# Two score banks in turn, and scores issued one step ahead, in the MLA stage of a two-layer kernel

## The chip, the cores and the metric

One core of a Trainium2 chip runs the whole program. The metric is the device time of one execution in microseconds (us); the median of 3 runs of the kernel before is 1999.83 us (1999.37 to 2000.95).

## The reference

Two transformer layers of different kinds over 512 tokens of width 1024. Only one part of the second layer is touched here: causal attention with latent projections (MLA), eight heads, computed in fp32 (`q`, `k` have 128 plain and 64 rotary features, `v` has 128):

```python
q = (rms(cq) @ w_uq).reshape(B, S, 8, 192)
kv = (rms(ckv) @ w_ukv).reshape(B, S, 8, 256); k_nope, v = kv[..., :128], kv[..., 128:]
k = concat([k_nope, broadcast(krope)]); q, k = rms(q), rms(k)      # then rotary on the last 64
s = einsum('bqhd,bkhd->bhqk', q_block, k) * 192 ** -0.5            # query blocks of 128, causal
mo = einsum('bhqk,bkhv->bqhv', softmax(s), v) @ w_bm
mixed = sigmoid(gr) * a_ret + sigmoid(gm) * mo                     # gr, gm = h @ parts of w_in
```

## The kernel before, in words

The program is written by hand for five in-order engines that meet only at semaphores. TensorE writes eight PSUM banks of 512 fp32 columns. Weights come from HBM in units into `raw`; ScalarE rounds a unit to `w_hi` (the high split), VectorE subtracts to make `w_lo` (the low split), and each product of weights is three matmuls (high x high, high x low, low x high).

The MLA stage (`mla`, one function of this name for each engine: L1299 on TensorE, L2123 on ScalarE, L3076 on VectorE) works on two heads at a time, in four rounds `i`. A round has eight steps `n`, one for each block of 128 queries and each of the two heads; `s = 8 * i + n`. The scores of step `n` have `(n // 2 + 1) * 128` columns, so steps 6 and 7 have 512. What a step does:

- TensorE (L1452 to L1475): `turn_p(s-1)` transposes the scaled probabilities of the step before; `scores(i, n)` writes bank 4; then transposes of new q or k tiles (`turn_q`, `turn_k`, bank 7); two pieces of weight work, `piece(i, 2n)` and `piece(i, 2n+1)`; and `weigh(s-1)`, probabilities times values.
- The pieces of rounds 0 to 2 prepare the next pair of heads: pieces 0 to 3 are quarters of gate `ga` (bank 2), 4 to 7 the four token tiles of the kv projection and 8 to 11 those of the q projection (banks 0 and 1 in turn), 12 to 15 quarters of gate `gb` (bank 3). A projection waits until the tile two before it has left its bank. In round 3 the 16 pieces are quarters of the four gates `gm`.
- VectorE (L3180 to L3223): `peak(s)` adds the causal mask in the bank and takes the row maximum; `scaled(s)` multiplies the exponentials with the inverse of their sum; `values` and `q_rope` take their parts of a projection out of its bank; `k_scaled`, `k_turned` scale and copy key tiles; `low` and `head_low` round outputs; `split` is the low split, in steps 0, 2, 4 and 7 (6 in round 3).
- ScalarE (L2210 to L2241): `high(s-2)` copies outputs, `projected` squares and copies a projection out of its bank, `fetch(s-1)` copies the transposed probabilities, `exp(s)` makes the exponentials out of bank 4 once `peak(s)` is done, then `q_turned`, `sigmoid` with table loads around it in step 1, and `split`.

In steps 3 and 4 VectorE's `values(i+1, 2n-5)` and in steps 5 and 6 its `q_rope(i+1, 2n-9)` stand ahead of `peak(s)`; on ScalarE the matching `projected` stands ahead of `fetch` and `exp(s)`. The next units after the stage (`merge2`) use banks 7, 4, 5, 6, 0, 1, 2 and 3.

## Time and profile before

| | us |
|---|---|
| median of 3 runs | 1999.83 |
| profiled execution, span | 1999.3 |
| TensorE busy | 1967.7 (98%) |
| VectorE busy | 1044.6 (52%) |
| ScalarE busy | 793.5 (40%) |
| MLA rounds (from the first scores to the last weighing) | 1309 to 1482 of the span |

Times in rows are counted from the span's start. A row of the timeline gives start, duration, engine, line, operation, tiles and shapes, and in brackets how long the engine had been idle before it and what ended that. A matmul's duration includes a tail that runs under the next ones; what it costs is the distance to the next start.

### The profile page before, as it was taken

The page shows a single profiled execution, that of the slowest core. Times are in us where ns is not written, and L with a number is a line of the kernel's source. Part 1 is how long each engine was busy: PE and PEld are TensorE (multiplying, and loading weights), DVE is VectorE, ACT ScalarE, POOL GpSimd, SP SyncE. Part 2 cuts the span into 40 slices and gives each one's busy share as a digit, 9 for nine tenths or more (in the row PEclk, how much of TensorE's full clock was granted, in tenths as well). Part 3 has the DMA queues.
Part 4 walks back from the last instruction along what each step waited for, and adds up shares of the span by engine and source line. Part 5 has one row for each costly group of instructions (what it writes and reads, how often), then busy time and mean ns, then how long its engine had stood idle before and what let it go on. Part 6 is the DMA issues. An engine that isn't in the chain of part 4 may idle for free.

```text
span 1999.3 us, 24017 instructions
## 1 busy us (share of the span) xinstructions
PE 1967.7 (98%) x9144; PEld 1594.7 (80%) x9144; DVE 1044.6 (52%) x1663; ACT 793.5 (40%) x1335; POOL 115.0 (6%) x138
## 2 busy tenths in 40 slices
PE   7999999999999999999999999999999999999998
PEld 6778777888888888877878787777778888888887
DVE  5687877455433544455353534466653553334354
ACT  5343556534222323333232323577752332322243
POOL 2140000002000000200000000000000200000011
PEclk9999999999999999999999999999999999999999
DMA  9842222123333332322223231211223332323321
GB/s 364 325 169 85 64 65 84 64 85 88 86 94 95 105 99 72 124 85 72 97 63 105 63 105 53 65 55 44 57 93 105 127 106 85 105 85 104 94 95 64
DMA packets 196578, 199.64 MB, mean 100 GB/s; under 512 B 7547, under 2 KB 170448, under 8 KB 194064
## 3 DMA queue, kind: packets, MB, share of 16 engines
q1 hardware_dynamic: 192416, 175.15, 28.2%
q0 software_dynamic: 4080, 23.40, 3.0%
q8 instruction: 51, 0.84, 0.2%
q14 instruction: 31, 0.25, 0.0%
HBM read 194.33 MB, written 4.19 MB: 99 GB/s over the span
## 4 chain that ended last, share of the span: by engine, by line
PE 90%; ACT 4%; DVE 3%; issue 1%; DMA 1%; SPq 0%; DVEq 0%; ACTq 0%
PE bank L761 47%; PE bank L1263 4%; PE bank L1014 4%; PE bank L851 4%; PE bank L837 3%; PE bank L1513 3%; PE bank L726 3%; PE bank L1333 2%; PE bank L1069 2%; PE bank L1241 2%; PE bank L881 1%; PE bank L998 1%; PE bank L964 1%; PE bank L1252 1%; PE bank L1283 1%
## 5 line engine op out<-in xcount | busy, mean ns | idle before, releaser
L1629 ACT ACTIVATE w_hi<-raw 128x2048 fp32r<-128x2048 f32 (+4 forms) x165 | 285.1, 1729 | 434.3 <-PE bank L761 306.6
L2372 DVE TENSOR_TENSOR w_lo<-raw,w_hi 128x2048 fp32r<-128x2048 f32 (+4 forms) x163 | 336.8, 2066 | 146.9 <-ACT w_hi L1629 145.0
L761 PE MATMUL bank<-h_hi,w_hi 128*128 128x512 f32 x864 | 337.7, 391 | 0.0
L761 PE MATMUL bank<-h_hi,w_lo 128*128 128x512 f32 x864 | 336.4, 389 | 0.0
L761 PE MATMUL bank<-h_lo,w_hi 128*128 128x512 f32 x864 | 336.1, 389 | 0.0
L761 PEld LDWEIGHTS bank<-h_lo,w_hi 128*128 128x128 f32 x864 | 162.2, 188 | 34.3 <-issue 0.5
L761 PEld LDWEIGHTS bank<-h_hi,w_lo 128*128 128x128 f32 x864 | 162.2, 188 | 34.0
L761 PEld LDWEIGHTS bank<-h_hi,w_hi 128*128 128x128 f32 x864 | 162.2, 188 | 34.0 <-issue 0.5
L761 PE MATMUL bank<-u_hi,w_hi 128*128 128x512 f32 x256 | 100.9, 394 | 0.0
L761 PE MATMUL bank<-u_hi,w_lo 128*128 128x512 f32 x256 | 100.4, 392 | 0.0
L761 PE MATMUL bank<-u_lo,w_hi 128*128 128x512 f32 x256 | 99.4, 388 | 0.0
L3311 DVE TENSOR_TENSOR xT<-bank,xT 128x512 f32<-128x512 f32 x32 | 22.1, 691 | 93.1 <-PE bank L761 92.5
L761 PE MATMUL bank<-g_hi,w_hi 128*128 128x512 f32 x176 | 69.4, 394 | 0.0
L761 PE MATMUL bank<-g_hi,w_lo 128*128 128x512 f32 x176 | 69.0, 392 | 0.0
L761 PE MATMUL bank<-g_lo,w_hi 128*128 128x512 f32 x176 | 68.3, 388 | 0.0
L1988 ACT ACTIVATE ft<-bank 128x512 f32<-128x512 f32 x22 | 13.2, 598 | 132.0 <-PE bank L761 125.7
L2856 DVE TENSOR_TENSOR ft<-bank,ft 128x512 f32<-128x512 f32 x22 | 15.2, 690 | 94.0 <-ACT ft L1988 94.0
L3299 DVE TENSOR_TENSOR nt<-nt 128x512 f32<-128x512 f32 x32 | 20.7, 688 | 77.3 <-ACT nt L2302 75.7
L2302 ACT ACTIVATE nt<-bank 128x512 f32<-128x512 f32 x32 | 17.4, 597 | 104.0 <-PE bank L761 104.0
L761 PEld LDWEIGHTS bank<-u_hi,w_lo 128*128 128x128 f32 x256 | 48.1, 188 | 11.3
L761 PEld LDWEIGHTS bank<-u_lo,w_hi 128*128 128x128 f32 x256 | 48.0, 188 | 10.8
L761 PEld LDWEIGHTS bank<-u_hi,w_hi 128*128 128x128 f32 x256 | 48.1, 188 | 9.6
(562 smaller groups left out, 4057.1 us busy)
## 6 DMA issues: line engine op xcount, KB each, us to landing
raw<-in_w_in SPq DMA_DIRECT2D x49, 1024.0 KB
raw<-in_w_ff SPq DMA_DIRECT2D x44, 512.0 KB
raw<-in_w_up SPq DMA_DIRECT2D x16, 1024.0 KB
raw<-in_w_down SPq DMA_DIRECT2D x16, 1024.0 KB
raw<-in_w_o SPq DMA_DIRECT2D x8, 1024.0 KB
raw<-in_w_br SPq DMA_DIRECT2D x8, 1024.0 KB
raw<-in_w_in SPq DMA_DIRECT2D x13, 512.0 KB
raw<-in_w_ff SPq DMA_DIRECT2D x8, 768.0 KB
```

The source lines that it names most:

```text
L726: last = nc.tensor.matmul(dst, a, b, start=n == 0, stop=n == len(terms) - 1)
L761: last = nc.tensor.matmul(dst, a, b, start=k == n == 0, stop=k == last_k and n == 2)
L837: last = nc.tensor.matmul(bank[t][:], a, b, start=half == k == n == 0, stop=half == 1 and k == 3 and n == 2)
L851: last = nc.tensor.matmul(bank[t][:], a, b, start=half == k == n == 0, stop=half == 1 and k == 3 and n == 2)
L1014: last = nc.tensor.matmul(bank[6 + n % 2][:], a, b, start=k == i == 0, stop=k == KD - 1 and i == 2)
L1069: last = nc.tensor.matmul(bank[2 * pair + m][:], a, b, start=k == i == 0, stop=k == 3 and i == 2)
L1241: last = nc.tensor.matmul(bank[4 + vt][:, j * P:S], rv[:, j, vt * P:vt * P + P], rs_t[:, j, 0:S - j * P], start=j == 0, stop=j == QT - 1)
L1263: last = nc.tensor.matmul(bank[OUT_BANK[half][n]][:], a, b, start=k == m == 0, stop=k == 3 and m == 2)
L1333: last = nc.tensor.matmul(bank[dst][:], a, b, start=k == n == 0, stop=k == KD - 1 and n == 2)
L1513: last = nc.tensor.matmul(bank[at][:], a, b, start=k == m == 0, stop=k == KD - 1 and m == 2)
L1629: nc.scalar.activation(w_hi[:, slot, 0:width], raw[:, slot, 0:width], ACT.Copy).then_inc(hi_done, 1)
L2372: v.tensor_tensor(w_lo[:, slot, 0:width], raw[:, slot, 0:width], w_hi[:, slot, 0:width].bitcast(F32), ALU.subtract).then_inc(lo_done, 1)
```

## The change

The scores alternate between banks 4 and 3. On TensorE, `scores(i, n+1)` is issued between the two pieces of step `n` (only the first scores of a round stay where they were) and waits for the exponential two steps before it instead of one. The transpose of the fourth key tile moves from ahead of the pieces of step 2 to behind them. Gate `gb` moves from bank 3 to bank 0, where it waits for the third q tile to have left, and the fourth `gm` gate from bank 3 to bank 7; the bank numbers of `merge2` follow. On ScalarE `exp(s)` is first in its step, then `high`, `fetch` and `projected`. On VectorE `peak(s)` is first in its step, ahead of `low`, `values` and `q_rope`, and each `k_turned(i, n)` stands in step `n` for 1 to 3. No instruction is added or taken away.

```diff
--- before.py
+++ after.py
@@ -358,7 +358,9 @@
         def x_copies(kind, j, t):
 
             return 2 + 20 * j + {"q": (3, 6, 9, 14), "k": (11, 16, 18, 20)}[kind][t]
-        GM_BANK = (2, 0, 1, 3)
+        GM_BANK = (2, 0, 1, 7)
+        GR_BANK = (2, 0)
+        S_BANK = (4, 3)
         SPLIT_STEPS = ((0, 2, 4, 7), (0, 2, 4, 7), (0, 2, 4, 7), (0, 2, 4, 6))
         kv_bank, q_bank = ((0, 1, 2, 3), (0, 1, 0, 1)), ((4, 5, 6, 0), (0, 1, 0, 1))
 
@@ -1313,6 +1315,8 @@
                         else:
                             pe.wait_ge(sem("kvq_act"), 3 * max(8 * j + t - 1, 8))
                             pe.wait_ge(sem("kvq_dve"), max(8 * j + t - 1, 8))
+                            if t == 0:
+                                pe.wait_ge(sem("gr_out"), 2 * j)
                         last = mm3(bank[kv_bank[j > 0][t]][:], tokens(lkv, t), [w_tile(u % 2, k, 512, 0, 512) for k in range(2)])
                     else:
                         if j:
@@ -1336,12 +1340,15 @@
 
                 def gr_piece(j, m, r):
                     if r == 0:
-                        if j:
-                            pe.wait_ge(sem("gr_out"), 2 * j - 1 + m)
+                        if m:
+                            pe.wait_ge(sem("kvq_act"), 3 * (8 * j + (7 if j else 8)))
+                            pe.wait_ge(sem("kvq_dve"), 8 * j + (7 if j else 8))
+                        elif j:
+                            pe.wait_ge(sem("gr_out"), 2 * j - 1)
                         else:
-                            pe.wait_ge(sem("kvq_act"), 3 * (3 + m))
-                            pe.wait_ge(sem("kvq_dve"), 3 + m)
-                    gate_quarter(u_mla(("ga", "gb")[m], j), 2 + m, r)
+                            pe.wait_ge(sem("kvq_act"), 3 * 3)
+                            pe.wait_ge(sem("kvq_dve"), 3)
+                    gate_quarter(u_mla(("ga", "gb")[m], j), GR_BANK[m], r)
 
                 def gm_piece(n, r):
                     if r == 0:
@@ -1350,8 +1357,9 @@
                         elif n == 1:
                             pe.wait_ge(sem("kvq_act"), 3 * 32)
                             pe.wait_ge(sem("kvq_dve"), 32)
+                            pe.wait_ge(sem("gr_out"), 8)
                         elif n == 3:
-                            pe.wait_ge(sem("gr_out"), 8)
+                            pe.wait_ge(sem("x_copied"), x_copies("k", 3, 3))
                     gate_quarter(U0["mla"] + 16 + n, GM_BANK[n], r)
 
                 def piece(i, n):
@@ -1396,10 +1404,11 @@
                 def scores(i, n):
                     t, hh = divmod(n, 2)
                     w = (t + 1) * P
-                    pe.wait_ge(sem("c_exp"), 8 * i + n)
+                    to = bank[S_BANK[n % 2]]
+                    pe.wait_ge(sem("c_exp"), max(8 * i + n - 1, 0))
                     pe.wait_ge(sem("x_copied"), max(x_copies("q", i, t), x_copies("k", i, t)))
-                    nc.tensor.matmul(bank[4][:, 0:w], qn[:, hh, t * P:t * P + P], kn[:, hh, 0:w], start=True, stop=False)
-                    nc.tensor.matmul(bank[4][:, 0:w], qr[:, hh, t * P:t * P + P], kr[:, 0:w], start=False, stop=True
+                    nc.tensor.matmul(to[:, 0:w], qn[:, hh, t * P:t * P + P], kn[:, hh, 0:w], start=True, stop=False)
+                    nc.tensor.matmul(to[:, 0:w], qr[:, hh, t * P:t * P + P], kr[:, 0:w], start=False, stop=True
                                      ).then_inc(sem("c_scores"), 1)
 
                 def turn_p(s):
@@ -1454,11 +1463,9 @@
                         s = 8 * i + n
                         if s:
                             turn_p(s - 1)
-                        scores(i, n)
                         if n == 0:
+                            scores(i, 0)
                             turn_q(i, 3)
-                        if n == 2:
-                            turn_k(i, 3)
                         if n == 5 and i < 3:
                             turn_q(i + 1, 0)
                         if n == 6 and i < 3:
@@ -1466,20 +1473,23 @@
                         if n == 7 and i < 3:
                             turn_q(i + 1, 2)
                         piece(i, 2 * n)
+                        if n < 7:
+                            scores(i, n + 1)
                         piece(i, 2 * n + 1)
                         if s:
                             weigh(s - 1)
-                        if n < 2:
+                        if n < 3:
                             turn_k(i, n + 1)
                         if n == 7 and i < 3:
                             turn_k(i + 1, 0)
 
                 def first_tile(k0, k1):
+                    pe.wait_ge(sem("c_exp"), 31)
                     for k in range(k0, k1):
                         pe.wait_ge(sem("heads_split"), k + 1)
                         a_hi, a_lo = w_tile(U0["merge2"] % 2, k, 256, 0)
                         for m, (a, b) in enumerate(((a_hi, mo_hi[:, k, :]), (a_hi, mo_lo[:, k, :]), (a_lo, mo_hi[:, k, :]))):
-                            nc.tensor.matmul(bank[7][:], a, b, start=k == m == 0, stop=False)
+                            nc.tensor.matmul(bank[4][:], a, b, start=k == m == 0, stop=False)
 
                 pe.wait_ge(lo_done, U0["merge2"] + 1)
                 first_tile(0, 3)
@@ -2158,7 +2168,7 @@
                 def sigmoid(j, m):
                     act.wait_ge(sem("gr_used"), max(2 * j + m - 1, 0))
                     act.wait_ge(mm_done, u_mla(("ga", "gb")[m], j) + 1)
-                    nc.scalar.activation(nt[:, 4 + m, :], bank[2 + m][:], ACT.Sigmoid).then_inc(sem("gr_out"), 1)
+                    nc.scalar.activation(nt[:, 4 + m, :], bank[GR_BANK[m]][:], ACT.Sigmoid).then_inc(sem("gr_out"), 1)
                 def exp_table(c):
                     nc.scalar.activation(warm[:, c:c + 1], eps[:], ACT.Exp)
 
@@ -2167,7 +2177,7 @@
                     act.wait_ge(sem("c_max"), s + 1)
                     act.wait_ge(sem("c_turned"), max(s - 1, 0))
                     w, n = (t + 1) * P, s % 8
-                    nc.scalar.activation(probs[:, s % 2, 0:w], bank[4][:, 0:w], ACT.Exp, bias=cst[:, 8 + n:9 + n],
+                    nc.scalar.activation(probs[:, s % 2, 0:w], bank[S_BANK[s % 2]][:, 0:w], ACT.Exp, bias=cst[:, 8 + n:9 + n],
                                          scale=inv[:, s // 8 % 2, 8 + 2 * t + hh:9 + 2 * t + hh], accum_out=cst[:, 16 + n:17 + n]
                                          ).then_inc(sem("c_exp"), 1)
 
@@ -2210,13 +2220,13 @@
                 for i in range(4):
                     for n in range(8):
                         s = 8 * i + n
+                        exp(s)
                         if s >= 2:
                             high(s - 2)
+                        if s:
+                            fetch(s - 1)
                         if i < 3 and 3 <= n <= 6:
                             projected(i + 1, "kv" if n < 5 else "q", (2 * n - 5) % 4)
-                        if s:
-                            fetch(s - 1)
-                        exp(s)
                         if n == 0:
                             q_turned(i, 3)
                         if 5 <= n <= 6 and i < 3:
@@ -3132,8 +3142,9 @@
                     t, hh = divmod(s % 8, 2)
                     w, n = (t + 1) * P, s % 8
                     dve.wait_ge(sem("c_scores"), s + 1)
-                    own.step(v.tensor_tensor(bank[4][:, t * P:w], bank[4][:, t * P:w], tri[:], ALU.add))
-                    own.step(v.tensor_reduce(cst[:, n:n + 1], bank[4][:, 0:w], axis=AX, op=ALU.max, negate=True))
+                    at = bank[S_BANK[s % 2]]
+                    own.step(v.tensor_tensor(at[:, t * P:w], at[:, t * P:w], tri[:], ALU.add))
+                    own.step(v.tensor_reduce(cst[:, n:n + 1], at[:, 0:w], axis=AX, op=ALU.max, negate=True))
                     v.tensor_tensor(cst[:, 8 + n:9 + n], cst[:, n:n + 1], inv[:, s // 8 % 2, 8 + 2 * t + hh:9 + 2 * t + hh],
                                     ALU.mult).then_inc(sem("c_max"), 1)
 
@@ -3180,7 +3191,8 @@
                 for i in range(4):
                     for n in range(8):
                         s = 8 * i + n
-                        if s >= 26 and n != 2:
+                        peak(s)
+                        if s >= 26:
                             low(s - 2)
                         if i < 3 and 3 <= n <= 4:
                             values(i + 1, 2 * n - 5)
@@ -3190,19 +3202,12 @@
                             sums(i + 1)
                         if n == 7 and i < 3:
                             inverse(i + 1)
-                        if n == 1:
-                            k_turned(i, 1)
-                        if n == 2:
-                            k_turned(i, 2)
-                            if i == 3:
-                                low(s - 2)
-                        peak(s)
+                        if 1 <= n <= 3:
+                            k_turned(i, n)
                         if n == 0:
                             k_scaled(i, 2)
                         if n == 1:
                             k_scaled(i, 3)
-                        if n == 2:
-                            k_turned(i, 3)
                         if n == 7 and i < 3:
                             k_scaled(i + 1, 0)
                         scaled(s)
...
```

## Rows read from the trace of the kernel before

**Rows 1.** Windows: length, busy PE, PEld, DVE, ACT, POOL, PE clock, DMA share, GB/s.
```profile
1356.00:1402.00 46.00, 43.91 (x234) 35.83 (x233) 29.02 (x99) 34.76 (x103) 0.00 (x0) 1.00 0.20 57
```

**Rows 2.** Waits of the stage: who, for whom, us in total, times, longest.
```profile
ACT nt L2170 <- DVE cst L3137: 42.1, 25, 3.0
...
PE bank L1409 <- DVE nt L3144: 3.5, 7, 0.8
```

**Rows 3.** Timeline of TensorE, rounds 0 and 1.
```profile
1310.33 0.50 PE L1333 MATMUL bank<-h_hi,w_hi 128*128 128x512 f32 x1
...
1355.14 0.47 PE L1333 MATMUL bank<-h_hi,w_hi 128*128 128x512 f32 x1 [0.84 <-DVE w_lo L2372]
...
1359.68 0.47 PE L1333 MATMUL bank<-h_hi,w_hi 128*128 128x512 f32 x1
...
1362.53 0.38 PE L1416 MATMUL bank<-nt,vv 128*128 128x128 f32 x2
...
1363.18 0.60 PE L1401 MATMUL bank<-kn,trigs 128*128 128x256 f32 x2
...
1364.05 0.51 PE L1394 MATMUL bank<-ident,kt 128*128 128x128 f32 x3
...
1369.67 0.39 PE L726 MATMUL bank<-w_hi,lat_lo 128*128 128x512 f32 x1
1370.15 0.47 PE L726 MATMUL bank<-w_hi,lat_hi 128*128 128x512 f32 x1
...
1373.47 0.64 PE L726 MATMUL bank<-w_hi,lat_hi 128*128 128x384 f32 x1
...
1380.86 0.34 PE L726 MATMUL bank<-w_hi,lat_hi 128*128 128x384 f32 x1
```

**Rows 4.** Timeline of ScalarE, the same rounds.
```profile
1311.77 0.46 ACT L2170 ACTIVATE nt<-bank,cst,inv 128x128 f32<-128x128 f32 x1
...
1362.68 1.08 ACT L2161 ACTIVATE nt<-bank 128x512 f32<-128x512 f32 x2
1363.78 1.28 ACT L2163 ACT_TABLE_LOAD   x1
...
1366.04 0.28 ACT L2138 ACTIVATE kt<-bank 128x128 f32<-128x128 f32 x1
...
1367.12 1.16 ACT L1629 ACTIVATE w_hi<-raw 128x1152 fp32r<-128x1152 f32 x1
...
1369.41 0.38 ACT L2178 ACTIVATE nt<-bank 128x256 f32<-128x256 f32 x1
...
1371.46 0.27 ACT L2138 ACTIVATE kt<-bank 128x128 f32<-128x128 f32 x1
...
1376.08 0.32 ACT L2138 ACTIVATE qt<-bank 128x192 f32<-128x192 f32 x1
...
1377.25 1.05 ACT L1629 ACTIVATE w_hi<-raw 128x1024 fp32r<-128x1024 f32 x1
```

**Rows 5.** Timeline of VectorE, round 1.
```profile
1359.41 0.42 DVE L3129 COPY kn<-bank 128x256 f32<-128x256 f32 x1
...
1359.96 0.30 DVE L3135 TENSOR_TENSOR bank<-bank,tri 128x128 f32<-128x128 f32 x1
...
1366.39 0.35 DVE L3144 TENSOR_SCALAR nt<-nt,cst 128x256 f32<-128x256 f32 x1
...
1368.31 1.36 DVE L2372 TENSOR_TENSOR w_lo<-raw,w_hi 128x1152 fp32r<-128x1152 f32 x1
1369.59 0.42 DVE L3083 COPY vv<-bank 128x256 f32<-128x256 f32 x1
1369.92 0.29 DVE L3135 TENSOR_TENSOR bank<-bank,tri 128x128 f32<-128x128 f32 x1
...
1374.30 0.29 DVE L3135 TENSOR_TENSOR bank<-bank,tri 128x128 f32<-128x128 f32 x1
...
1377.39 0.29 DVE L3092 TENSOR_TENSOR turned_q<-bank,q_tabs 128x128 f32<-128x128 f32 x1 [0.56 <-ACT qt L2143]
```

More of the change, by code:

```diff
@@ L1495, in first_unit @@
                 def first_unit():
-                    for n, dst in enumerate((7, 4)):
+                    for n, dst in enumerate((4, 3)):
                         for k in range(6 * (n == 0), KD):
@@ L1520, in merge2_mm @@
                 pe.wait_ge(sem("gm_out"), 4)
-                unit(u + 3, (2, 3), mo)
+                unit(u + 3, (2, 7), mo)
                 pe.wait_ge(sem("mixed"), KD + 2)
-                unit(u + 4, (7, 4), h)
+                unit(u + 4, (4, 3), h)
                 pe.wait_ge(sem("mixed"), KD + 4)
@@ L2272, in merge2_epi @@
                 for n in range(2):
-                    sigmoid(nt[:, n, :], (7, 4)[n], mm_done, u + 5)
+                    sigmoid(nt[:, n, :], (4, 3)[n], mm_done, u + 5)
                 split(u + 6)
@@ L3243, in merge2_epi @@
                 dve.wait_ge(sem("gr_used"), 8)
-                mixed(u, 0, 7, gm[:, 0, :])
-                mixed(u, 1, 4, gm[:, 1, :])
+                mixed(u, 0, 4, gm[:, 0, :])
+                mixed(u, 1, 3, gm[:, 1, :])
                 split(u + 2)
@@ L3255, in merge2_epi @@
                 mixed(u + 3, 4, 2, nt[:, 0, :])
-                mixed(u + 3, 5, 3, nt[:, 1, :])
+                mixed(u + 3, 5, 7, nt[:, 1, :])
                 v.memset(small[:, 22:23], 0.0).then_inc(banks_free, 25)
```

## Prediction

> **What bounds the kernel now.** I read the table of windows first. In the MLA stage TensorE is the bound: in one round of 46 us it is busy 43.91 us at granted clock 1.00, VectorE 29.02 and ScalarE 34.76 [rows 1]. The change can only win back the remainder, some 2 us a round. The waits name it: ScalarE's exponential waits 42.1 us for the row maximum, which costs nothing by itself, and TensorE's transpose of the probabilities (`turn_p`, L1409) waits 3.5 us in 7 places for the scaled probabilities [rows 2]. The real delay is longer than such a row says. A 512-wide matmul is shown as 0.39 us but the next one starts 0.23 us later, so about 0.17 us of each idle gap is hidden under the last matmul's tail [rows 3]. The seven waits are then 3.5 + 7 x 0.17 = 4.7 us: about 0.96 before step 7 of rounds 0 to 2, 0.9 in two places of round 0 and 0.9 in two places of round 3.
>
> Three other losses are in a round. Piece 7 (the fourth kv projection) starts at 1370.15, 0.48 after its predecessor instead of 0.23, so 0.25 late; the first q matmul (1373.47) shows 0.64 us where its neighbours have 0.34, so 0.30 late [rows 3]. The first gate piece of the next round waits 0.84 (really 1.1) for `w_lo` at 1355.14.
>
> I call that piece start T0 and give all times of rounds 1 and 2 from it; steps are counted 0 to 7, a step has pieces 2n and 2n+1, and p7 is piece 7. The same piece starts 44.07 us apart in rounds 1, 2 and 3; the first of the three is shown [rows 3].
>
> **What is removed.** With scores(n+1) issued between the pieces of step n, the maximum, exponential and scaling of head-step n have one and a half steps of TensorE work as cover, instead of one. All seven `turn_p` waits go: -4.7 us. The late p7 and p8 are replaced by what I find below, so I take their 0.55 a round off as well, in round 0 too, though it may have up to 0.5 more there. The wait for `w_lo` at T0 stays. It hangs on `turn_k` of the next round, which ends a round: `k_turned`, `k_scaled` and the low split follow it on VectorE in the same order as before.
>
> **What is added on TensorE.** No matmul is new. A scores block costs 0.87 us at 256 columns (1363.18 to 1364.05 [rows 3]), so 0.43 per 128 columns. A switch from a narrow fp32 matmul to a weight piece costs 0.09: twelve matmuls of 0.23 are 2.76, and the pair of pieces from 1359.68 to 1362.53 took 2.85. After scores in the middle there is one switch more where they are narrow (three in a round), and one where `turn_p` now stands directly before the piece (step 4, and steps 4 to 7 of round 3): 3 x 4 + 7 = 19 x 0.09 = 1.7 us. Its bounds are 0 and 28 x 0.09 = 2.5. The Trainium skill (TensorE: Matmul & The Clock Gate, Step-by-step) says that TensorE pulls weight loads ahead of running matmuls. Taken alone it would make the switches free and the sum 1.7 lower; the 0.09 measured at 1359.68 speaks against that for narrow matmuls.
>
> **What is moved on ScalarE and VectorE.** This is the costly part. `exp(s)` now stands first in ScalarE's step and `peak(s)` first in VectorE's. The evacuation that TensorE needs for bank 1, `projected(kv,1)` on ScalarE and `values(1)` on VectorE, stood ahead of them in step 3. Now it stands behind `exp(3)`, thus behind `peak(3)`, thus behind the low split that ends VectorE's step 2, thus behind the high split that ends ScalarE's step 2. p7 writes bank 1 and waits for it. I follow this chain from the end of p3, the last piece of gate a, which ScalarE's sigmoid waits for:
> - matmul tail 0.17, one sigmoid 0.54 (half of 1.08), exp table, mo copy, fetch and exp(2) together 2.26 (1363.78 to 1366.04), projected(kv,0) 1.08 (1366.04 to 1367.12), high split 1.16 [rows 4]: 5.21
> - low split and its hand-over 0.04 + 1.28 (1368.31 to 1369.59), peak(3) and exp(3) with their hand-over 1.54 (1369.92 to 1371.46) [rows 4, 5]: 2.86
> - mo copy 0.16, fetch(2) 0.28 (0.38 less the usual overlap of 0.1), projected(kv,1) 1.08 and 0.12 to VectorE, values 0.42 and 0.14 to TensorE (1369.59 to 1370.15) [rows 3 to 5]: 2.20
> Sum 10.3 us. TensorE took 1370.15 - 0.25 - 1362.53 = 7.37 from the end of p3 to p7; now scores(2) (0.87) lies before it, scores(4) (1.30) within it, and three switches more: 8.07. **p7 starts 2.2 us late**, in each of the rounds 0, 1 and 2.
>
> From there the two engines take turns. Counted from values(1), p7 starts at 0.56. VectorE: values(1) 0.34, the copies of the last key tile 0.55 (1359.41 to 1359.96), scaled(3) 0.47 (0.35 at 1366.39 and its short reciprocal), values(2) 0.34, then peak(4) and exp(4) 1.78 (1374.30 to 1376.08): 3.48. ScalarE: copies 0.16 + 0.28, projected(kv,3) 1.08, q0 1.17 (1376.08 to 1377.25), high split 1.05: 7.22. VectorE: low split 0.04 + 1.14 (1.28 less an eighth, as it is narrower), peak(5) and exp(5) 1.78: 10.2. ScalarE: copies 0.16 + 0.38, projected(q,1) until VectorE starts 1.31 (1376.08 to 1377.39), then q_rope 0.88 and 0.14 to TensorE: 13.0 [rows 4, 5]. p11, the fourth q piece, waits for exactly this. TensorE from p7 to p11 was 10.71 (1370.15 to 1380.86), less 0.30 of waiting, less scores(4) 1.30, plus scores(6) 1.73 and 0.18: 11.0, so it is ready at 11.6. **p11 starts 1.4 us late.** Behind it there is slack: gate b's bank 0 is free by its step, and turn_p(6) and the key transpose that end the round come 0.4 to 0.5 us later than what they wait for.
>
> A third, smaller one: scores(2) needs the second key tile half a step earlier. Its copy started at T0 + 4.27 (1359.41), right behind the low split of step 0 [rows 5]. Now two more ScalarE copies (0.64) stand before that split, and peak(1) (0.74, an estimate: 1.54 less the exponential of 0.56, the hand-over of 0.1 and the narrower reduction's 0.13) before the copy itself (0.62 to its end, and 0.14 to TensorE): 6.41. TensorE is there at 4.54 (1359.68) + 1.43 + 0.15 = 6.12: 0.3 late. In round 0 exp(0) starts 1.44 after T0 (1310.33 to 1311.77 [rows 3, 4]) instead of the 0.62 of the other rounds, two copies and one `weigh` of 0.88 on TensorE are missing: 0.3 + 0.82 - 0.64 + 0.88 = 1.35 late.
>
> The Trainium skill (same page, Architectural detail) states that ScalarE and VectorE are strict FIFO. By that rule nothing overtakes the waiting `peak` or `exp`, as in the chains; the trace agrees: ScalarE sits idle ahead of exponentials 42.1 us.
>
> **The other moves cost nothing.** Gate b in bank 0 waits for q2's evacuation, out by the above before p12; kv0 in bank 0 waits for the sigmoid of gate b, which runs in the idle time before gate a's. Moving the fourth key tile to step 3 leaves it two steps before scores(6). Weight loads from HBM start at the low splits, later by at most the stalls, and in this stage no high split waits for a transfer. The last units only change bank names.
>
> **The sum.** Rounds 1 and 2: -0.96 - 0.55 + 0.3 + 2.2 + 1.4 + 0.1 (p9, which is due just as bank 1 comes free) + 0.36 (4 switches) = +2.85 each. Round 0: -0.96 - 0.9 - 0.55 + 1.35 + 2.2 + 1.4 + 0.1 + 0.36 = +3.0. Round 3 has no projections, hence no p7 or p11 stall: -0.9 + 0.3 + 0.6 = 0. Together +8.7 us. The profiled span is 1999.33 and the median of the runs 1999.83, 0.5 apart, so 1999.8 + 8.7 = **2008.5**.
>
> **Rivals.**
> 1. The stalls of the score chain go and none comes: ScalarE and VectorE run far enough ahead that p7 and p11 aren't late. It decides on whether the chain after p3 is under 8.07 instead of 10.3, and the next under 11.0. For it: both engines are idle over a fifth of the round. Against: the chain begins with a sigmoid that can't start before p3 ends. Then -4.7 - 1.65 + 1.7 = -4.6, **1995.2**; with the late scores(2) (1.3 + 3 x 0.3 = 2.2) kept, 1997.4. The Trainium skill (Perfetto Trace Analysis, Matmuls) advises to rotate independent matmul groups through different PSUM banks so that evacuation overlaps the next group; by that rule this rival is what happens. The trace bears it out for the score bank and against it for bank 1, whose evacuation is queued later. Chance 0.15.
> 2. Only the first stall is real, and p11's is absorbed, for instance since projected(q,1) is early: 8.7 - 3 x 1.4 = +4.5, **2004.3**. Chance 0.15.
> 3. The lag isn't made good by the end of a round, and reaches the next round's low split and turn_p(6) (margin 0.5) again: 1 to 2 us more a round, **2013**. Chance 0.08.
> My forecast, the three late starts as priced, within 2005 to 2012: 0.62.
>
> Range 1997 to 2012: it takes in rival 2, the upper half of rival 1's spread (the late scores(2), all switches priced), the bounds of the switches, and an error of 1 us a round on the chains. A measurement of this kernel can tell 0.2%, 4.0 us, from no change. Faster than 1995.8 needs rival 1 nearly whole: 0.08. Between: the rest of it and half of rival 2, 0.19. Slower: 0.73.
>
> **What the profile after would show.** The `turn_p` waits gone; instead L726 waiting for VectorE's `vv` copy (L3083 before) some 2 us, three times, and for q_rope's output (L3098 before) some 1.3 us, three times; a scores wait on `kr` in step 1; rounds of about 46.9 us where they were 44.06, round 3 unchanged. ScalarE's wait for the maximum concentrated in steps 3, 4 and 5, behind the splits. The forecast is wrong if p7 starts without a wait, or if the round is under 45 us.

## The result, and the profile after

The changed kernel took **2009.39 us** (median of four runs, 2008.39 to 2009.99), the kernel before 2000.37 (four runs, 1999.37 to 2000.95). The ratio is **1.0046 [1.0031, 1.006]**: slower by 9.0 us. Single executions of one kernel lie in two groups some 1.5 us apart (1999.4 and 2000.9 for the kernel before) that differ ahead of this stage (round 0 begins at 1308.6 to 1308.9 us of the span in the profiles of the lower group, at 1310.1 to 1310.6 in the others), so a difference of medians is good to about 0.7 us, and the lengths of the rounds tell it more exactly. In the page's summary (busy time, share of the span, instructions) TensorE's busy time is what it was, 1968.3 against 1967.7 us; the span grew from 1999.3 to 2008.2.

```profile
span 2008.2 us, 24023 instructions
...
PE 1968.3 (98%) x9144; PEld 1595.1 (79%) x9144; DVE 1042.3 (52%) x1663; ACT 791.8 (39%) x1335; POOL 115.0 (6%) x138
```

The windows of the four rounds, from first gate piece to first gate piece and for round 3 to the first tile of the next stage (columns as in [rows 1]):

```profile
1310.14:1357.75 47.61, 41.51 (x216) 33.40 (x217) 28.48 (x96) 33.23 (x96) 0.00 (x0) 1.00 0.15 46
1357.75:1405.19 47.44, 42.37 (x225) 34.32 (x225) 27.67 (x95) 32.61 (x97) 0.00 (x0) 1.00 0.17 46
1405.19:1452.65 47.46, 42.38 (x224) 34.30 (x225) 27.67 (x95) 32.61 (x97) 0.00 (x0) 1.00 0.17 47
1452.65:1490.60 37.95, 37.76 (x190) 30.09 (x190) 25.48 (x71) 21.51 (x49) 0.00 (x0) 1.00 0.34 103
```

Cut in the same way, the rounds before were 44.81, 44.07, 44.07 and 38.49 us. The changes are +2.80, +3.37, +3.39 and -0.54: together +9.0, which is the whole result. The waits name the places. First TensorE's own (who, for whom, us in total, times, longest; they answer to [rows 2]):

```profile
PE bank L728 <- ACT kt L2148: 6.9, 3, 2.3
PE bank L728 <- DVE qt L3108: 4.1, 3, 1.4
...
PE bank L1337 <- DVE w_lo L2382: 2.5, 3, 0.8
...
PE bank L1410 <- ACT nt L2180: 1.8, 4, 1.2
```

and the largest of all engines within the stage, ScalarE's exponential waiting for the maximum, where it was 42.1:

```profile
ACT nt L2180 <- DVE cst L3148: 54.8, 24, 3.5
```

L728 is the projection (L726 before), L1337 a gate piece, L1410 the first scores matmul. `turn_p` (L1418 now) is in no row: its seven waits are gone. Two rows of the projection took their place, 6.9 us in three and 4.1 us in three. TensorE in round 1, whose T0 is now 1357.75 (these rows answer to [rows 3]):

```profile
1357.75 0.47 PE L1337 MATMUL bank<-h_hi,w_hi 128*128 128x512 f32 x1 [0.84 <-DVE w_lo L2382]
...
1364.12 0.67 PE L1410 MATMUL bank<-kn,trigs 128*128 128x256 f32 x2 [0.19 <-ACT nt L2180]
...
1366.44 0.38 PE L1425 MATMUL bank<-nt,vv 128*128 128x128 f32 x2
...
1373.75 0.81 PE L1411 MATMUL bank<-kr,trigs 128*128 128x384 f32 x2
...
1376.87 0.47 PE L728 MATMUL bank<-w_hi,lat_hi 128*128 128x512 f32 x1 [2.31 <-ACT kt L2148]
...
1387.14 1.02 PE L1411 MATMUL bank<-kr,trigs 128*128 128x512 f32 x2
1389.52 0.41 PE L728 MATMUL bank<-w_hi,lat_hi 128*128 128x384 f32 x1 [1.36 <-DVE qt L3108]
```

p7 starts at 1376.87, 19.12 after T0, and its gap of 2.31 us is longer in truth: the scores matmuls of 1373.75 (384 columns) would have let it start at 1374.40, had they cost the 0.65 that the same pair takes to the next start at 1380.57; that makes it **2.47 us** late (the piece behind the pair at 1381.22 comes 0.72 later, but that piece is late itself, as the part on the mis-sized terms shows). p11 starts at 1389.52, 31.77 after T0, **1.52 us** late, scores(2) at 1364.12 are 0.36 late. The name of a releaser needs care: the row of 1364.12 names an exponential, but the one that scores(2) wait for was long over; what had just ended was the copy of the key tile (VectorE, L3140, 1363.69 + 0.28 = 1363.97).

The chain to p7 on ScalarE (answering to [rows 4, 5]):

```profile
1366.70 0.60 ACT L2171 ACTIVATE nt<-bank 128x512 f32<-128x512 f32 x1 [0.43 <-PE bank L1337]
1367.31 1.28 ACT L2173 ACT_TABLE_LOAD   x1
...
1370.66 1.16 ACT L1639 ACTIVATE w_hi<-raw 128x1152 fp32r<-128x1152 f32 x1
1374.10 0.56 ACT L2180 ACTIVATE nt<-bank,cst,inv 128x256 f32<-128x256 f32 x1 [2.29 <-DVE cst L3148]
...
1375.88 0.38 ACT L2153 ACTIVATE kt<-bank 128x256 f32<-128x256 f32 x1
```

and VectorE's part of it:

```profile
1371.85 1.36 DVE L2382 TENSOR_TENSOR w_lo<-raw,w_hi 128x1152 fp32r<-128x1152 f32 x1 [0.37 <-ACT w_hi L1639]
1373.12 0.29 DVE L3146 TENSOR_TENSOR bank<-bank,tri 128x128 f32<-128x128 f32 x1
...
1376.30 0.42 DVE L3093 COPY vv<-bank 128x256 f32<-128x256 f32 x1 [2.23 <-ACT kt L2153]
```

Sigmoid, table, exp(2), high split (1370.66) on ScalarE; low split (1371.85) and peak(3) (1373.12) on VectorE; exp(3) (1374.10), the copy of the projection (1375.88) on ScalarE; values(1) (1376.30) on VectorE; p7. Each starts when the one before it has ended; between exp(3) and the copy of the projection stand only two short copies and the projection's own two squares (`projected` squares a tile twice, L2148, and then copies it, L2153).

### The profile page after: what moved, and what is told of

Same layout as the page of the kernel before. It is cut to its first block, busy times and chain, and to the rows that moved or that the text cites. A ratio compares the mean times of both kernels' runs of the same rounds, so it can differ in the third digit from the quotient of the medians.

```text
span 2008.2 us, 24023 instructions
## 1 busy us (share of the span) xinstructions
PE 1968.3 (98%) x9144; PEld 1595.1 (79%) x9144; DVE 1042.3 (52%) x1663; ACT 791.8 (39%) x1335; POOL 115.0 (6%) x138
## 4 chain that ended last, share of the span: by engine, by line
PE 90%; ACT 4%; DVE 4%; issue 1%; DMA 1%; SPq 0%; ACTq 0%; DVEq 0%
PE bank L763 47%; PE bank L1265 4%; PE bank L1016 4%; PE bank L853 4%; PE bank L839 3%; PE bank L728 3%; PE bank L1523 3%; PE bank L1337 2%; PE bank L1071 2%; PE bank L1243 2%; PE bank L883 1%; PE bank L1000 1%; ACT w_hi L1639 1%; PE bank L966 1%; PE bank L1254 1%
## 5 line engine op out<-in xcount | busy, mean ns | idle before, releaser
L763 PEld LDWEIGHTS bank<-u_lo,w_hi 128*128 128x128 f32 x256 | 48.1, 188 | 10.8
```

The costliest lines, as they stand in the source:

```text
L763: last = nc.tensor.matmul(dst, a, b, start=k == n == 0, stop=k == last_k and n == 2)
```

## Experiments

The question is what makes p7 and p11 late: the shared bank, the order on ScalarE, the order on VectorE, or the place of the scores.

### 1. The evacuation ahead of exp again, on both engines or on ScalarE alone

e1 moves `projected` ahead of `exp` and `values`/`q_rope` ahead of `peak` in steps 3 to 6; e2 makes only ScalarE's move:

```diff
                         s = 8 * i + n
+                        if i < 3 and 3 <= n <= 6:
+                            projected(i + 1, "kv" if n < 5 else "q", (2 * n - 5) % 4)
                         exp(s)
...
-                        if i < 3 and 3 <= n <= 6:
-                            projected(i + 1, "kv" if n < 5 else "q", (2 * n - 5) % 4)
```
e1 has this on VectorE besides:
```diff
-                        peak(s)
-                        if s >= 26:
-                            low(s - 2)
                         if i < 3 and 3 <= n <= 4:
...
                             q_rope(i + 1, 2 * n - 9)
+                        peak(s)
+                        if s >= 26:
+                            low(s - 2)
```

> The kernel after, with one edit on each of two engines: in steps 3 to 6 of rounds 0 to 2 the evacuations (projected on ScalarE, values and q_rope on VectorE) stand ahead of exp and peak again. Banks and TensorE's order stay. Theory A (queued-behind chain: p7 and p11 wait because the evacuation stands behind exp and peak): the three waits of 2.3 us before p7 and the three of 1.4 us before p11 go; about 0.4 us comes back before p8, since kv2 is then due just after it. A round falls from 47.44 us to about 43.8, the kernel to 1998 to 1999.5. Theory B (the scores between the pieces cost the time by themselves, through switches of TensorE or the earlier need of the second key tile): 2007 to 2009, as the kernel after.

> The kernel after with ScalarE's edit of the run before alone; VectorE's values and q_rope stay behind peak. Theory A1 (ScalarE's queue is the link that matters: the projection's evacuation waits behind exp, exp waits for peak, peak for the low split): projected(kv,1) runs straight after the high split of step 2, values(1) is at T0 + 16.1 to 16.5 and p7 is ready at 16.8, so again 1998 to 1999.5. Theory A2 (VectorE's order is the link): values(1) behind peak(3) still holds p7, a wait of 1 us or more before p7 and p11 stays, 2003 or more.

Measured: **e2 1998.63 us, 0.9988 [0.9979, 0.9998]**; e1 2006.37, 1.0024 [1.0013, 1.0034]. The one move on ScalarE is worth 2009.39 - 1998.63 = 10.8 us (11.4 by the rounds, which are 43.82, 43.65, 43.66 and 37.96 in e2). In e2 the row for p7 and the row for p11 are gone and no row of waits came in their place; what is left there are starts that are 0.18 to 0.27 us late under the tail of the matmul ahead (p6, p7 and p8 of round 1). ScalarE of e2 shows why: the projection is taken straight behind the high split (its first square starts at 1366.72), and exp(3) still waits 1.22 us for its maximum after that, so the move cost the exponential nothing.

```profile
1365.66 1.16 ACT L1639 ACTIVATE w_hi<-raw 128x1152 fp32r<-128x1152 f32 x1
1366.72 0.27 ACT L2148 ACTIVATE kt<-bank 128x128 f32<-128x128 f32 x1
...
1369.12 0.56 ACT L2180 ACTIVATE nt<-bank,cst,inv 128x256 f32<-128x256 f32 x1 [1.22 <-DVE cst L3148]
```

e1 fell outside both expectations. p7 and p11 are on time there, but three others are late. TensorE's waits of e1:

```profile
PE bank L1337 <- ACT qt L2148: 2.3, 3, 0.8
...
PE bank L728 <- ACT kt L2148: 1.8, 3, 0.6
```

and VectorE's timeline of e1 in step 3 of round 1:

```profile
1372.26 0.42 DVE L3093 COPY vv<-bank 128x256 f32<-128x256 f32 x1
1372.59 0.29 DVE L3146 TENSOR_TENSOR bank<-bank,tri 128x128 f32<-128x128 f32 x1
```

The rows are gate b's first piece (0.77 late in round 1), and p8 (0.60); a weighing in step 7 waits 0.52 besides. With `values(1)` (1372.26) ahead of it, peak(3) begins at 1372.59, behind a copy. In steps 5 and 6 it is worse: `q_rope` waits for ScalarE's copy, and peak, which could have run meanwhile, waits with it; then exp waits for peak, and the copies behind exp wait for exp. The two engines run one after the other instead of side by side. So in the changed kernel the two moves have opposite signs: taking back exp's move on ScalarE gains 10.8 us, taking back peak's as well loses most of them again: 7.7 by the medians (2006.37 - 1998.63), 7.3 by the rounds (46.26, 46.07, 46.07 and 37.96 in e1).

### 2. A third bank instead

The tiles of the projections go through banks 0, 1 and 2 instead of 0 and 1 (bank 2 is free between the gates), everything else as in the changed kernel, apart from the waits that go with it:

```diff
-        kv_bank, q_bank = ((0, 1, 2, 3), (0, 1, 0, 1)), ((4, 5, 6, 0), (0, 1, 0, 1))
+        kv_bank, q_bank = ((0, 1, 2, 3), (0, 1, 2, 0)), ((4, 5, 6, 0), (1, 2, 0, 1))
...
-                            pe.wait_ge(sem("kvq_act"), 3 * max(8 * j + t - 1, 8))
+                            pe.wait_ge(sem("kvq_act"), 3 * max(8 * j + t - 2, 8 * j))
```

> The kernel after with three banks in turn (0, 1, 2) for the eight projection tiles of a pair instead of two, so that each piece waits for the tile three before it; all orders stay. Theory A (the chain through both engines is the bound, and the bank only the place where TensorE meets it): the waits before p7 and p11 go, but turn_p(4), turn_q(0) and p12, which need the same chain, take about 0.7, 0.8 and 1.3 us of waiting instead; 2006.5 to 2009, a gain of 0 to 3 us. Theory C (two banks are too few): all of 12 us comes back, 1997.5.

Measured: 2008.40 us, 1.0040 [1.0026, 1.0054], as theory A said. The waits of p7 and p11 are gone, and the time is all but the same, since others wait instead (waits, then one row of TensorE's timeline):

```profile
PE bank L1424 <- DVE nt L3161: 5.0, 5, 1.6
PE bank L1339 <- issue: 3.1, 4, 0.8
```

```profile
1377.99 0.44 PE L1424 MATMUL bank<-ident,nt 128*128 128x128 f32 x2 [1.55 <-DVE nt L3161]
```

L1424 is `turn_p`, L1339 a gate piece; the wait of 1.55 us at 1377.99 is for the scaled probabilities that ScalarE and VectorE had not yet reached. One more bank only lets TensorE run up to the next thing that the same late chain delivers. (The expectation put the wait one `turn_p` later than it stands.)

### 3. One step at a time

e7 puts `projected` ahead of `exp` in step 3 alone; e6 leaves the order and moves the split of the q weights, which stands in the chain to p7, from step 2 to step 3:

```diff
+                        if i < 3 and n == 3:
+                            projected(i + 1, "kv", 1)
                         exp(s)
...
-                        if i < 3 and 3 <= n <= 6:
+                        if i < 3 and 4 <= n <= 6:
```
```diff
-        SPLIT_STEPS = ((0, 2, 4, 7), (0, 2, 4, 7), (0, 2, 4, 7), (0, 2, 4, 6))
+        SPLIT_STEPS = ((0, 3, 4, 7), (0, 3, 4, 7), (0, 3, 4, 7), (0, 2, 4, 6))
```

> The kernel after with ScalarE's evacuation ahead of exp in step 3 alone (projected(kv,1)); steps 4 to 6 keep exp first. Theory A: p7's three waits of 2.3 us go, p11's stay at 1.1 to 1.5, the kernel is at 2001 to 2003. If p7's lateness covers another one (TensorE would only wait later), p11's wait grows by what p7's shrinks and the time stays at 2007 to 2009.

> The kernel after with the split of the q weights moved from the end of step 2 to the end of step 3 in rounds 0 to 2, on both engines. It takes 1.16 and 1.28 us out of the chain from the end of p3 to p7 and puts them into the chain from there to p11. If the chain is as written, the 2.3 us wait before p7 shrinks to under 0.3, p8 waits about 0.8 for the low split, and p11's wait grows from 1.4 to 2.3 or more; the time stays within 1.5 us of the kernel after. If the wait before p7 has another cause than the splits ahead of peak(3), it stays at 2.3.

Measured: e7 2006.41, 1.0028 [1.0016, 1.0040]; e6 2010.25, 1.0051 [1.0035, 1.0067]. TensorE of e7 in round 1:

```profile
1377.95 0.42 PE L728 MATMUL bank<-w_hi,lat_hi 128*128 128x384 f32 x1 [0.66 <-ACT qt L2148]
...
1385.54 0.41 PE L728 MATMUL bank<-w_hi,lat_hi 128*128 128x384 f32 x1 [1.37 <-DVE qt L3110]
```

and of e6:

```profile
1373.84 0.47 PE L728 MATMUL bank<-w_hi,lat_hi 128*128 128x512 f32 x1 [0.60 <-ACT kt L2148]
...
1377.03 0.44 PE L728 MATMUL bank<-w_hi,lat_hi 128*128 128x384 f32 x1 [0.89 <-DVE w_lo L2382]
...
1380.89 0.41 PE L728 MATMUL bank<-w_hi,lat_hi 128*128 128x384 f32 x1 [0.74 <-ACT qt L2148]
...
1388.48 0.41 PE L728 MATMUL bank<-w_hi,lat_hi 128*128 128x384 f32 x1 [1.40 <-DVE qt L3108]
```

In e7 p7 shows no wait, but p9 (1377.95) now waits 0.66 us and p11 (1385.54) still 1.37: of the 7.4 us that three late starts at p7 cost, 3.0 came back by the medians and 3.8 by the rounds (46.37, 46.16, 46.15), between the two figures that were expected. p11's lateness is its own, not p7's handed on. In e6 the wait of 2.31 at p7 became 0.60, 0.89 and 0.74 at p7, p8 and p9, and p11 comes 32.05 us after T0 (1356.43) instead of 31.77. So the wait at p7 shrank, as the chain demands, but not to the 0.3 that was expected, and p11's wait did not grow to 2.3: p8 and p9 took it up. Taking the split out of the one chain put it into the next: a round is as long as the work that ScalarE and VectorE do in turn, not as the one wait that shows.

### 4. The place of the scores and the second bank

e11 is the changed kernel with `scores(i, n)` back at the start of its own step (two banks, new orders). e4 is the kernel before with the new orders (one bank, `exp` first, `peak` first). e8 is the kernel before with `peak` first on VectorE alone.

```diff
+                        scores(i, n)
                         if n == 0:
-                            scores(i, 0)
...
                         piece(i, 2 * n)
-                        if n < 7:
-                            scores(i, n + 1)
```
e4, on ScalarE, against the kernel before:
```diff
+                        exp(s)
                         if s >= 2:
                             high(s - 2)
-                        if i < 3 and 3 <= n <= 6:
-                            projected(i + 1, "kv" if n < 5 else "q", (2 * n - 5) % 4)
                         if s:
                             fetch(s - 1)
-                        exp(s)
+                        if i < 3 and 3 <= n <= 6:
+                            projected(i + 1, "kv" if n < 5 else "q", (2 * n - 5) % 4)
```
e4 and e8, on VectorE:
```diff
+                        if n == 1:
+                            k_turned(i, 1)
+                        if n == 2:
+                            k_turned(i, 2)
+                        peak(s)
+                        if s >= 26:
                             low(s - 2)
...
-                        peak(s)
```

> The kernel after with both score banks and both orders kept, but scores(i, n) at the start of step n as before. With e4_order_alone (2045.7) it tells which part of TensorE's change keeps the new order from costing 45 us. Theory P (the place: issued a step ahead, the scores are finished before the evacuation that they queue ahead of is wanted): 2040 to 2047, as e4. Theory Q (the second bank, which lets the scores be written before the exponential of the step before is read): near the kernel after, 2009 to 2015.

> The kernel before with the new order alone: exp first in ScalarE's step, and peak ahead of low, values and q_rope in VectorE's; one score bank, scores at the start of their step. Theory A: p7 is 2.9 us late and p11 2.0 us late in three rounds, less the 0.55 of waits that they replace, and turn_p still waits: 1999.8 + 3 x 4.35 = 2013, between 2010 and 2015. Theory B (the scores' new place costs the time): 1999 to 2001.

> The kernel before with VectorE's order alone changed: peak(s) ahead of low, values and q_rope; one score bank, scores in their old place, ScalarE as before. It asks whether e2_act_only's gain over the kernel before is the two banks' or only VectorE's order. Theory A (the gain is the early scores'): turn_p(6)'s 0.96 goes three times, since peak(6) no longer stands behind q_rope, but p7 and p11 become some 0.9 and 0.3 us later three times: 1999 to 2002. Theory D (VectorE's order is the gain): 1997 to 1998.6.

| scores | ScalarE: projection behind exp | ScalarE: projection ahead of exp |
|---|---|---|
| a step ahead, two banks | 2009.39 (after) | 1998.63 (e2) |
| at the start of their step | 2045.64 (e11, two banks), 2045.68 (e4, one bank) | 2001.00 (e8, one bank; ratio 1.0001 [0.9991, 1.0010]) |

`peak` stands ahead of the evacuations on VectorE in all of them; in e8 `high` and `fetch` stand ahead of exp as well. e8 by itself changes nothing: the `turn_p` waits fall from 3.5 us in 7 places to 0.5 in 2, and p7 waits up to 1.0 us for `values`, which now stands behind `peak`. The ratio of e11 is 1.0224 [1.0208, 1.0239], that of e4 1.0225 [1.0208, 1.0242]. e4 missed its expectation by over 30 us: I had priced the lateness of p7 and p11 only. With the scores at the start of the step the ring closes: the copy out of the bank waits for exp, exp for peak, peak for the scores, and these for the late piece ahead of them on TensorE. The waits of e4's stage:

```profile
DVE bank L3135 <- PE bank L1402: 39.2, 18, 4.2
...
PE bank L726 <- ACT kt L2138: 10.9, 3, 3.6
PE bank L726 <- DVE qt L3098: 8.4, 3, 2.8
```

and a window of e11 that covers its round 1, and behind it the row of p7 in that round, of TensorE's timeline:

```profile
1369.00:1428.00 59.00, 46.56 (x224) 37.67 (x224) 28.30 (x95) 32.50 (x97) 0.00 (x0) 0.91 0.14 37
```

```profile
1388.25 0.76 PE L728 MATMUL bank<-w_hi,lat_hi 128*128 128x512 f32 x1 [3.61 <-ACT kt L2146]
```

VectorE waits 39.2 us in 18 places for scores. e11 and e4 agree to 0.04 us: **in the change's order the second bank by itself is worth nothing, and the place that it allows is worth 36 us**. Part of the 36 is a lower clock: over the four rounds TensorE is busy 178.07 us in e11 and 164.01 in the changed kernel, with the same matmuls (see the last part). With the projection ahead of exp, place and bank together (and with them the banks of the gates and the order of `high` and `fetch`, which differ between e8 and e2 too) are worth 2.4 (2001.00 against 1998.63); no run takes these apart.

### 5. What is left of e2's waits: the key copies

e2's remaining waits are `w_lo` at T0 (2.5 us, 3 times) and scores(2) (1.8, 4 times). e5 moves `k_turned(i, 1)` ahead of the low split of step 0, and `k_scaled(i+1, 1)` behind the low split of step 7. e9 leaves the splits first, puts `k_turned(i, 1)` ahead of peak(1), and moves `k_scaled(i, 1)` behind peak(0) of the next round; e10 makes that last move alone, in the kernel before.

```diff
                         s = 8 * i + n
+                        if n == 1:
+                            k_turned(i, 1)
                         peak(s)
...
                         if n == 0:
+                            if i:
+                                k_scaled(i, 1)
                             k_scaled(i, 2)
...
                             k_turned(i + 1, 0)
-                            k_scaled(i + 1, 1)
```

> The version of e2_act_only (ScalarE's evacuations ahead of exp, all else as after) with two more moves on VectorE: the copy of the second key tile goes from step 1 to the end of step 0, ahead of the low split, and the scaling of the next pair's second key tile goes behind the low split of step 7. What e2_act_only still waits for is scores(2) on the key copy (1.39 in round 0, 0.36 in rounds 1 to 3) and the first gate piece of a round on the low split (1.08 three times). Theory A (each of these is what ends its wait): 2.5 and 3 x 0.72 = 2.2 us go, 1998.6 becomes 1993 to 1995. Rival (the next thing on VectorE or ScalarE is late just behind them): 1997 or more.

> The version of e2_act_only with two moves on VectorE, placed where VectorE has nothing to wait for: the copy of the second key tile stands ahead of peak(1), still behind the low split of step 0, and the scaling of the next pair's second key tile moves from step 7 to step 0 of the round that needs it, behind peak(0), where VectorE was idle 2.0 us. Theory: e5_two_copies lost because its copy stood ahead of the low split and waited for TensorE's transpose, which held up peak(1), exp(1) and gate b's sigmoid; here 3 x 0.72 of the low-split wait at T0 and 3 x 0.36 + 0.7 of the scores(2) wait go, 3.9 us: 1994 to 1996 beside 1998.6. If exp(1), now 0.55 later, holds the sigmoid past piece 4: 1996 to 1998.

> The kernel before with one of these moves alone: the scaling of the next pair's second key tile behind peak(0). The low split at T0 comes 0.72 earlier in three rounds: 2000.9 - 2.2 = 1998.7, if nothing else ends the wait of 1.1 at T0; exp(0) is not delayed. So 1998 to 1999.5.

Measured: e5 1999.84, 0.9995 [0.9986, 1.0004]; **e9 1996.55, 0.9979 [0.9970, 0.9988]**; e10 1998.77, 0.9990 [0.9981, 0.9999]. VectorE of e5:

```profile
1358.15 0.42 DVE L3139 COPY kn<-bank 128x256 f32<-128x256 f32 x1 [2.30 <-PE bank L1402]
...
1358.69 1.22 DVE L2382 TENSOR_TENSOR w_lo<-raw,w_hi 128x1024 fp32r<-128x1024 f32 x1
1359.82 0.29 DVE L3146 TENSOR_TENSOR bank<-bank,tri 128x128 f32<-128x128 f32 x1
```

TensorE of e5, at p4:

```profile
1363.61 0.47 PE L728 MATMUL bank<-w_hi,lat_hi 128*128 128x512 f32 x1 [1.08 <-ACT nt L2171]
```

TensorE's waits of e9:

```profile
PE bank L1410 <- DVE kr L3140: 1.6, 4, 0.5
...
PE bank L1337 <- ACT nt L2171: 0.8, 1, 0.8
```

In e5 the copy stood first, waited 2.30 us for its transpose, and held up the low split and peak(1) behind it, thus exp(1) and the sigmoids; p4, which needs gate b's bank, waited 1.08 us, a gate piece of round 3 waited 1.7 for gate b's sigmoid, and the gain was gone, as the rival said. In e9 the same copy stands behind the split, where its transpose is ready. The row for `w_lo` at T0 is no longer in e9's list nor in e10's, and e10's round is 43.36 (T0 at 1352.93 and 1396.29) instead of 44.07: 3 x 0.71 = 2.1 us, beside 2.04 between the medians (2000.81 and 1998.77). e9 beats the kernel before by 4.3 us and the changed one by 12.8. What it has left is 0.8 us at a gate piece of round 3, which waits for gate b's sigmoid, and the key copies' 1.6. Against e2 it gained 2.1 us where up to 3.9 was expected: the first three rounds fell to 42.94, 42.90 and 42.93, but round 3 grew from 37.96 to 38.51.

## Why the prediction held, point by point

The mechanism is the one that was forecast, and the runs show it: late evacuations at p7 and p11. That the total came within 0.3 us (+9.0 against +8.7) is partly luck: the sum took away 1.0 us too little, added 2.9 too little for late starts and 1.7 for switches that cost nothing, and these cancel. This is the ledger of the four rounds, summed from the distances between starts in both traces. A start counts as late by what it exceeds the usual distance (0.23 us behind a 512-column piece matmul, 0.17 behind a 384-column one, 0.11 for each 128 columns of every other record; a row with x2 holds two records), and the first matmul behind a wait takes 0.07 to 0.08 more than its like, which belongs to the price.

| us, all rounds | forecast | in the traces |
|---|---|---|
| late starts taken away | -6.3 | -7.3 |
| late starts added | +13.4 | +16.2 |
| switches | +1.7 | 0 |
| sum | +8.7 | +8.9 |

- **What is removed.** All seven `turn_p` waits went, and so did the late start at p7; `w_lo` at T0 stayed at 0.84 (2.5 in three), as said. The second "late" piece, p8, was misread: in the kernel before, the scores matmul of 384 columns starts at 1373.12 and the second matmul of p8 at 1373.94, and 0.82 is just 0.65 + 0.17. The first matmul of p8 was not late; its record only begins early. What was late there was `turn_p(3)`, by 0.18. Round 0 had 0.8 more to lose than the sum took (the prediction said up to 0.5).
- **p7, forecast 2.2, measured 2.47.** The three parts of the chain were forecast at 5.21, 2.86 and 2.20. Measured they are 5.38 (p3's end at 1366.44 to the high split's end, 1370.66 + 1.16), 2.83 (to 1374.65, where exp(3) is done) and 2.22 (to 1376.87): 10.43. TensorE reached the place 7.96 after p3's end, not 8.07 (the three switches in that sum cost nothing, and a late start of p6, 0.18, is in the 7.96). Both misses point the same way. The first part's miss is the second sigmoid: from p3's end to the table load at 1367.31 are 0.87 where 0.17 + 0.54 = 0.71 was taken from half of a back-to-back pair.
- **p11, forecast 1.4, measured 1.52.** From values(1) 13.22 instead of 13.0, TensorE 11.70 instead of 11.6.
- **scores(2), forecast 0.3 and 1.35 in round 0, measured 0.36 and 1.39.**
- **Mis-sized terms.** Rounds 1 and 2 came 0.5 longer than the +2.85 of the sum. With the 0.07 or 0.08 behind each wait, p7 costs 0.34 more than its term, p11 0.20 and scores(2) 0.13. p9, priced at 0.1, shows no wait but is 0.15 late: its bank comes free when values(3) ends at 1381.79, and it starts at 1381.94. p6 is late in the same hidden way, by 0.18 (it starts at 1371.62, values(0) ends at 1371.48), and is not in the sum at all. That is 0.9 more, less 0.36 for switches that cost nothing. Round 0 came at +2.80 against +3.0, round 3 at -0.54 against 0.
- **The switches.** This term was mis-sized: 1.7 forecast, nothing measured. The 0.09 came from the first matmul of a piece, which takes 0.31 to the next start instead of 0.23. But it starts only 0.03 behind the start of the last narrow matmul, which alone costs 0.11. Over both, nothing is lost (round 0 of the changed kernel):

```profile
1311.64 0.38 PE L1410 MATMUL bank<-kn,trigs 128*128 128x128 f32 x2
1311.86 0.39 PE L1411 MATMUL bank<-kr,trigs 128*128 128x128 f32 x2
1312.00 0.48 PE L1337 MATMUL bank<-h_hi,w_hi 128*128 128x512 f32 x1
1312.31 0.39 PE L1337 MATMUL bank<-h_lo,w_hi 128*128 128x512 f32 x1
```

  A pair of narrow matmuls takes 0.22 (1311.64 to 1311.86), and pair and first piece matmul together take 0.45 (1311.86 to 1312.31) = 0.22 + 0.23. The kernel before has the same at the place that the prediction read: 0.45 from 1359.54 to 1359.99. It holds for wide scores too: step 5 of round 3 takes 4.83 in the kernel before (1465.10 to 1469.93) and 5.25 in the changed one (1475.20 to 1480.45), which has one switch more and 0.43 more of scores. So the prediction's 0.09 against free switches does not stand, and round 3 comes out to within 0.1: 1.06 us of `turn_p` waits went, 0.43 at scores(2) came, and the 0.6 of switches never did.
- **The rivals.** The first (no late start) is refuted by the row of p7. e2 comes near to it: 1998.63, where 1995.2 to 1997.4 was forecast; late scores(2) and the hidden late starts of p6, p7 and p8 remain in it. The second fell with e7, in which p7 shows no wait and p11 is late all the same. The third (lag carried over) fell with the rounds: 47.61, 47.44, 47.46 with no growth, and `w_lo` at T0 unchanged at 0.84.
- **The advice on banks.** The Trainium skill (Perfetto Trace Analysis, Matmuls) advises independent matmul groups in different banks. By e3, with a third bank and the time unchanged at 2008.40, and by e11 and e4, two banks and one at 2045.6, it gave nothing here by itself, as long as the evacuation stood behind exp.

What was only argued: that the order inside e1's steps 5 and 6 explains the gate's wait (0.8 in three) was read from the timeline, and not tried apart.

## What to carry to other kernels

Before an exponential or any dependent work is put first in an in-order queue, ask which instruction behind it frees a buffer for the bound engine, and follow the chain to that instruction through every engine; if the dependent work would wait anyway, the evacuation goes ahead of it for nothing (10.8 us here for one line on ScalarE). The rule isn't symmetric: on the engine that feeds the chain (VectorE's maximum) the chain's work goes first, and work that waits for the other engine goes behind (7.3 us here with early scores; with late ones, in e8, that order changed nothing). A further buffer, or a split moved out of one chain changed here which wait shows, and hardly the length of the round; compare the round's length, not the wait. And read a cost over both sides of a boundary: a matmul that seems slow may only have begun early.

## What the runs showed of the hardware

The change of TensorE's clock was in no expectation. In e11 round 1 took 58.60 us (T0 at 1369.66 and 1428.26), 11.2 more than in the changed kernel, and of that about 4 were busy time: 224 matmuls in 46.56 us instead of 225 in 42.37, with a granted clock of 0.91 over the window, a mixture of the levels 2.4 and 1.2 GHz. In its rounds TensorE waited up to 3.61 us at once. In e4, behind a wait of 3.63 us:

```profile
1387.44 0.47 PE L726 MATMUL bank<-w_hi,lat_hi 128*128 128x512 f32 x1 [3.63 <-ACT kt L2138]
...
1389.20 1.06 PE L1416 MATMUL bank<-nt,vv 128*128 128x128 f32 x4
...
1390.48 1.49 PE L1401 MATMUL bank<-kn,trigs 128*128 128x384 f32 x2
```

The first four matmuls after the wait still run at full pace (0.23 to 0.31 apart), the `weigh` of four at 1389.20 takes 1.06 us (0.61 in the changed kernel at 1378.34, after a wait of 2.31) and the two scores at 1390.48 1.49 (0.81); the granted clock from 1389.20 to 1391.00 is 0.50, the lower level, and from 1392.70 on the pace is full again. In e11, behind a wait of the same length (3.61, the row of 1388.25 above), already the first matmul takes 0.56 to the next start and the following ones 0.43. In the changed kernel, with waits of 2.31 and 1.36 in a round, the granted clock of all four rounds is 1.00. No run tells which length or which sum of waits makes the difference.
